# Strassen block products for the up and gate chunks of five feed-forward stages

## Chip, cores and metric

The kernel runs on one core of a Trainium2 chip. The metric is the device time of one execution in microseconds (us). Five compute engines take part: TensorE (PE, with its weight loads shown as PEld), VectorE (DVE), ScalarE (ACT), GpSimd (POOL) and SyncE (SP), which here issues the weight transfers.

## The reference

Four layers of width 1024 on 512 tokens in float32. Two of them end in a squared-relu feed-forward part, the other two have a SwiGLU feed-forward part ahead of the mixer and one behind it. What the change touches is the first matrix product of each:

```python
def _sq_relu_mlp(h, w_up, w_down):            # 1024 -> 4096 -> 1024
    u = jax.nn.relu(h @ w_up)
    return (u * u) @ w_down

def swiglu(x, w_gu, w_d):                     # 1024 -> 2 x 2816 -> 1024
    ...
    return (jax.nn.silu(gate) * up) @ w_d

def second_block(...):
    for i in range(DEPTH):                    # 2
        x = x + 0.5 * rms_norm(swiglu(rms_norm(x, g[0]), ffn_wgu[i, 0], ffn_wd[i, 0]), g[1])
        ...
        x = x + 0.5 * rms_norm(swiglu(rms_norm(x, g[4]), ffn_wgu[i, 1], ffn_wd[i, 1]), g[5])
```

## The kernel before

Every product is made of three: each operand is split into a rounded part (`hi`) and a rest (`lo`), and `three` issues hi·hi, hi·lo and lo·hi as three matmuls into one PSUM bank. The weights come from memory in chunks of 1 MB: 1024 rows by 256 columns for an up or gate chunk, 256 rows by 1024 columns for a down chunk. A chunk passes four engines. SP issues its load into one of two slots of `raw` (L291). ACT copies it to `whi` (L299), DVE subtracts to get `wlo` (L305), and PE multiplies it (`pe_chunk`, L309 to L311). `whi` and `wlo` have two slots too. The load of chunk n+2 waits until DVE has made `wlo` of chunk n, and ACT's copy of chunk n+2 waits until PE has finished chunk n.

The stages run in the order of PLAN: rg, f0, nsa, f1, s00, even, s01, s10, odd, s11, with a norm ahead of each, and post and store at the end. f0 and f1 are the squared-relu parts (16 groups of 256 columns, each one up chunk and one down chunk). The four s stages are the SwiGLU parts (11 groups of a gate chunk, an up chunk and a down chunk). `ffn_walk` fixes the order for every engine: gate and up of groups 0 and 1, down of 0, gate and up of 2, down of 1, and so on. Each engine runs its own program in that order and meets the others at semaphores.

In a gate or up chunk, PE makes two tiles of 128x512 (48 matmuls). DVE evicts a gate tile with a multiplication by `rstd` (L476), ACT takes silu (L426), POOL multiplies by `rstd` again (L458), DVE multiplies the up tile by that (L491), ACT rounds the product to `u_hi` (L434) and DVE makes `u_lo` (L496). In f1 the eviction is a relu (L480), and ACT squares. A down chunk is eight tiles of six matmuls. Tile m goes to bank m mod 4 of the half of PSUM that its group owns, DVE adds each to `fsum` or `x` (L517), and tile m=4 to 7 may start only when the add of tile m−4 is done, since it takes the same bank. The norms between the stages (L585 to L820) have PE, ACT, DVE and POOL work tile by tile; `pool_owed` (L687) is POOL's part there. `pool_even_early` and `pool_odd_early` prepare constants in `arena` for the mixers even and odd. POOL runs them ahead of its part of s00 and s10.

Of the kernel before, what the change touches and what calls it, by code (L numbers as in the profile page):

```python
# [20 lines left out]
P = 128  # L21
# [20 lines left out]
def build(nc, a, out):  # L42
    ctx = ExitStack()
    with ctx:
# [68 lines left out]
        LEFT, RIGHT = slice(0, S // 2), slice(S // 2, S)  # L113
        s_pe = sem("s_pe")
# [59 lines left out]
        def swi(l, i):  # L174
# [4 lines left out]
            return dict(gu=2, groups=NG2, w=[g, u], down=down, swiglu=True, dst=fsum)  # L179

# [87 lines left out]
        owed_no = {i: sum(s_[0] in ("norm", "post") and s_[1] is not None for s_ in PLAN[:i]) for i in range(len(PLAN))}  # L268
        swi_base = {n_: b_ - sum(FFN[m_]["groups"] for m_ in FFN if not FFN[m_]["swiglu"]) for n_, b_ in ffn_base.items()}
# [76 lines left out]
        def ffn_walk(e, name, gu, dn):  # L346
            f = FFN[name]
            G, per = f["groups"], f["gu"] + 1
            n0 = where[name]

            def n_gu(g):
                return n0 if g == 0 else n0 + f["gu"] + (g - 1) * per

            def n_dn(g):
                return n0 + f["gu"] + g * per + f["gu"] if g < G - 1 else n0 + G * per - 1
# [3 lines left out]
            dt = 2 * (2 * f["gu"] + 8)  # L359
            gu(0, n_gu(0), None, 0, 0)  # L360
            for g in (1, 2):
                gu(g, n_gu(g), None, 0, 0)
# [54 lines left out]
        def act_ffn(e, name):  # L417
            f, b, bs = FFN[name], ffn_base[name], swi_base[name]

            def gu(g, n, i, dn, dt):  # L420
                if f["swiglu"]:
# [28 lines left out]
            ffn_walk(e, name, gu, down)  # L450

        def pool_ffn(e, name):
            b = swi_base[name]

            def gu(g, n, i, dn, dt):
                for j in range(2):
                    e.wait_ge(silu_done, at(2 * (b + g) + j + 1, i, 4))
                    e.tensor_tensor(tmp[:, j, :], tmp[:, j, :], rstd[:, :], ALU.mult).then_inc(scaled, 1)  # L458
# [3 lines left out]
            ffn_walk(e, name, gu, down)  # L462

        def dve_ffn(e, name, stage):
# [3 lines left out]

            def gu(g, n, i, dn, dt):
                half = 4 * (g % 2)  # L470
# [22 lines left out]
                for j in range(2):  # L493
                    e.wait_ge(uhi_done, at(2 * (b + g) + j + 1, i, 4))
                    u = 2 * (g % 2) + j
                    e.tensor_tensor(u_lo[:, u, :], tmp[:, 2 + j, :], u_hi[:, u, :].bitcast(F32),  # L496
                                    ALU.subtract).then_inc(ulo_done, 1)
# [3 lines left out]
            def down(g, n, i, dn, dt):  # L501
                final = i is None and g == f["groups"] - 1
                half = 4 * (g % 2)
                for m in range(8):
                    if m == 4 and not final:
                        dve_lo(e, n + 1, i, dn, dt)
                    e.wait_ge(tiles_out, at(before[n] + m + 1, i, dt))
# [2831 lines left out]
```

## Time and profile before

| what | value |
|---|---|
| median of 3 runs | 3573.53 us (3571.29 to 3574.26) |
| span of the profiled execution | 3570.0 us |
| PE busy | 3490.7 us, 98% of the span |
| PEld busy | 2787.9 us, 78% |
| DVE busy | 1950.1 us, 55% |
| ACT busy | 1247.5 us, 35% |
| POOL busy | 439.1 us, 12% |

The span is one profiled execution, and the times of the runs contain some 3.5 us around it. A matmul's row shows the time from its start to its modelled end, and matmuls overlap, so PE's pace is read from the distance between starts.

### The profile page before, as it was taken

How to read it: one execution, taken by the hardware profiler on the slowest of the kernel's cores; microseconds unless marked ns; L12 is line 12 of the kernel's file. 1: busy time of each engine (PE TensorE's matmuls, PEld its weight loads, DVE VectorE, ACT ScalarE, POOL GpSimd, SP SyncE). 2: the span in 40 equal slices, each digit the busy share in tenths (PEclk: the TensorE clock that was granted, in tenths of full speed). 3: DMA queues.
4: the chain of work that ended last, by engine and by line, in shares of the span. 5: the costliest groups of instructions: out<-in, count | busy, mean ns of one | idle time of the engine just before them, and what ended most of it. 6: DMA issues, size and time to landing. Idle time of an engine off the chain costs nothing.

```text
span 3570.0 us, 47147 instructions
## 1 busy us (share of the span) xinstructions
PE 3490.7 (98%) x18751; PEld 2787.9 (78%) x18751; DVE 1950.1 (55%) x2686; ACT 1247.5 (35%) x1776; POOL 439.1 (12%) x351
## 2 busy tenths in 40 slices
PE   8999999999999999999999999999999999999998
PEld 6888888645888878887777788878888777778887
DVE  5655563465555565446577555555545534465545
ACT  5632232465422242223644422233223422243222
POOL 1220002010100021112023011111111000011101
PEclk9999999899999999999999999999999999999999
DMA  3332334100222222233100132323222222223231
GB/s 119 106 111 94 94 94 95 36 1 24 95 94 94 94 96 95 94 98 97 59 26 24 52 106 94 100 77 106 94 94 95 83 83 87 79 66 100 96 104 60
DMA packets 232554, 295.92 MB, mean 83 GB/s; under 512 B 21893, under 2 KB 201464, under 8 KB 232392
## 3 DMA queue, kind: packets, MB, share of 16 engines
q1 hardware_dynamic: 230864, 290.48, 25.6%
q0 software_dynamic: 1152, 3.05, 0.4%
q8 instruction: 115, 1.88, 0.2%
q14 instruction: 47, 0.39, 0.0%
q10 hardware_dynamic: 376, 0.12, 0.0%
HBM read 291.53 MB, written 2.10 MB: 82 GB/s over the span
## 4 chain that ended last, share of the span: by engine, by line
PE 90%; DVE 5%; ACT 3%; issue 1%; DMA 0%; SPq 0%; DVEq 0%; ACTq 0%
PE bank L309 26%; PE bank L311 26%; PE bank L310 26%; PE bank L338 1%; PE bank L340 1%; PE bank L339 1%; PE bank L3057 1%; DVE wlo L305 1%; PE bank L2458 1%; PE bank L1585 1%; PE bank L1500 1%; PE bank L1569 1%; ACT whi L299 1%; ACT fsum L1666 1%; PE bank L1599 0%
## 5 line engine op out<-in xcount | busy, mean ns | idle before, releaser
L309 PE MATMUL bank<-h_hi,whi 128*128 128x512 f32 x2748 | 1083.1, 394 | 22.2 <-DVE h_lo L789 9.9
L311 PE MATMUL bank<-h_hi,wlo 128*128 128x512 f32 x2748 | 1069.5, 389 | 0.0
L310 PE MATMUL bank<-h_lo,whi 128*128 128x512 f32 x2748 | 1069.3, 389 | 0.0
L299 ACT ACTIVATE whi<-raw 128x2048 fp32r<-128x2048 f32 x266 | 508.6, 1912 | 1245.1 <-PE bank L311 1192.7
L305 DVE TENSOR_TENSOR wlo<-raw,whi 128x2048 fp32r<-128x2048 f32 x266 | 612.9, 2304 | 323.5 <-ACT whi L299 323.4
L309 PEld LDWEIGHTS bank<-h_hi,whi 128*128 128x128 f32 x2748 | 517.0, 188 | 147.2 <-issue 31.4
L310 PEld LDWEIGHTS bank<-h_lo,whi 128*128 128x128 f32 x2748 | 517.1, 188 | 107.1 <-issue 3.6
L311 PEld LDWEIGHTS bank<-h_hi,wlo 128*128 128x128 f32 x2748 | 516.9, 188 | 107.4
L309 PE MATMUL bank<-u_hi,whi 128*128 128x512 f32 x1440 | 562.0, 390 | 4.6 <-DVE arena L3133 2.4
L310 PE MATMUL bank<-u_lo,whi 128*128 128x512 f32 x1440 | 560.8, 389 | 0.0
L311 PE MATMUL bank<-u_hi,wlo 128*128 128x512 f32 x1440 | 560.7, 389 | 0.0
L309 PEld LDWEIGHTS bank<-u_hi,whi 128*128 128x128 f32 x1440 | 270.4, 188 | 63.7 <-issue 4.3
L311 PEld LDWEIGHTS bank<-u_hi,wlo 128*128 128x128 f32 x1440 | 270.4, 188 | 56.2
L310 PEld LDWEIGHTS bank<-u_lo,whi 128*128 128x128 f32 x1440 | 270.4, 188 | 56.0 <-issue 0.2
L458 POOL TENSOR_TENSOR tmp<-tmp,rstd 128x512 f32<-128x512 f32 x88 | 175.4, 2014 | 1118.1 <-ACT tmp L426 1117.8
L517 DVE TENSOR_TENSOR fsum<-fsum,bank 128x512 f32<-128x512 f32 x316 | 212.1, 685 | 85.9 <-PE bank L311 84.8
L517 DVE TENSOR_TENSOR x<-x,bank 128x512 f32<-128x512 f32 x255 | 169.0, 683 | 51.7 <-PE bank L311 51.7
L491 DVE TENSOR_TENSOR tmp<-bank,tmp 128x512 f32<-128x512 f32 x88 | 60.8, 691 | 246.3 <-PE bank L311 210.8
L476 DVE TENSOR_TENSOR tmp<-bank,rstd 128x512 f32<-128x512 f32 x88 | 60.1, 690 | 229.2 <-PE bank L311 214.5
L434 ACT ACTIVATE u_hi<-tmp 128x512 fp32r<-128x512 f32 x88 | 55.7, 632 | 327.3 <-DVE tmp L491 327.3
L480 DVE SCALAR_TENSOR_TENSOR tmp<-bank,rstd 128x512 f32<-128x512 f32 x64 | 44.1, 691 | 181.3 <-PE bank L311 181.3
L438 ACT ACTIVATE tmp<-tmp 128x512 f32<-128x512 f32 x64 | 40.4, 632 | 256.6 <-DVE tmp L480 256.6
(441 smaller groups left out, 3095.6 us busy)
## 6 DMA issues: line engine op xcount, KB each, us to landing
raw<-in_ffn_wgu SPq DMA_DIRECT2D x88, 1024.0 KB, 5.0
raw<-in_ffn_wd SPq DMA_DIRECT2D x44, 1024.0 KB, 4.9
raw<-in_mlp_w_up SPq DMA_DIRECT2D x32, 1024.0 KB, 5.7
raw<-in_mlp_w_down SPq DMA_DIRECT2D x32, 1024.0 KB, 4.8
raw<-in_odd_w_in SPq DMA_DIRECT2D x24, 1024.0 KB, 5.1
raw<-in_even_w_in SPq DMA_DIRECT2D x13, 1024.0 KB, 5.3
raw<-in_rg_w_in SPq DMA_DIRECT2D x8, 1024.0 KB, 5.6
raw<-in_odd_w_out SPq DMA_DIRECT2D x8, 1024.0 KB, 5.0
```

The costliest lines, as they stand in the source:

```text
L299: e.activation(whi[:, n % 2, :], raw[:, n % 2, :], ACT.Copy).then_inc(hi_ready, 1)
L305: e.tensor_tensor(wlo[:, n % 2, :], raw[:, n % 2, :], whi[:, n % 2, :].bitcast(F32), ALU.subtract).then_inc(lo_ready, 1)
L309: pe.matmul(o, w_hi, r_hi, start=first, stop=False)
L310: pe.matmul(o, w_hi, r_lo, start=False, stop=False)
L311: return pe.matmul(o, w_lo, r_hi, start=False, stop=last)
L434: e.activation(u_hi[:, u, :], tmp[:, 2 + j, :], ACT.Copy).then_inc(uhi_done, 1)
L438: e.activation(tmp[:, 2 + j, :], tmp[:, j, :], ACT.Square)
L458: e.tensor_tensor(tmp[:, j, :], tmp[:, j, :], rstd[:, :], ALU.mult).then_inc(scaled, 1)
L476: ins = e.tensor_tensor(tmp[:, j, :], pbank[half + j][:, :], rstd[:, :], ALU.mult)
L480: ins = e.scalar_tensor_tensor(tmp[:, j, :], pbank[half + j][:, :], 0.0, rstd[:, :], ALU.max, ALU.mult)
L491: e.tensor_tensor(tmp[:, 2 + j, :], pbank[half + 2 + j][:, :], tmp[:, j, :], ALU.mult)\
L517: e.tensor_tensor(dst[:, m, :], dst[:, m, :], src[:, :], ALU.add).then_inc(added, 1)
```

## The change

In f1, s00, s01, s10 and s11 the up and gate chunks from group 3 on (13 chunks in f1, 16 in each s stage, 77 in all) are computed as a 2x2 block product by Strassen's scheme in Winograd's form: seven products of half the size in each dimension instead of eight. A chunk (1024 rows, 256 columns) is cut in four quarters of 512 rows and 128 columns, and the tokens in two halves of 256. One such product is 4 blocks of rows by 3 matmuls of 128x256, so a chunk is 84 matmuls of 128x256 (`pe_seven`) in place of 48 of 128x512.

The sums that the scheme needs are spread over the engines. POOL makes four sums of weights per chunk, each waiting for the one before (`pool_weights`, L444 to L450 of the new program, one of them written into `raw`); ACT then copies 2048 elements to `whi` and 1536 to `x_hi`, and DVE makes `wlo` and `x_lo` (L466). The token sums are made once per stage, from 8 DVE products, 8 POOL sums, 4 ACT copies and 4 DVE subtractions of 1792 elements, and stand in `th`, which lies in `arena`. `rstd` is already in the tokens, so POOL's scaling (L458) goes in these groups. The seven products are joined on the way out of PSUM: ACT copies the first to `snap`, and DVE adds tiles of 256 columns.

In the down chunks DVE makes `wlo` of the next chunk ahead of add m=1 instead of m=4, `x_lo` of the next gate chunk and both `u_lo` ahead of add m=3. Since `th` needs `arena`, `pool_even_early` and `pool_odd_early` move into the norm ahead of even and odd, behind `pool_owed`.

```diff
+        SEVEN = {"f1": 3, "s00": 3, "s01": 3, "s10": 3, "s11": 3}
+        def seven(name, g):
+            return name in SEVEN and SEVEN[name] <= g < FFN[name]["groups"]
...
+        PRODUCTS = (("m", 0, 0, TB11, 0), ("x", XS2, 0, T2, 1), ("x", XS3, 0, T3, 2), ("m", 0, 1, T1, 3),
+                    ("m", 4, 0, TB21, 0), ("m", 4, 1, T4, 2), ("x", XS4, 0, TB22, 3))
+        P_A, P_B, P_E, P_C, P_A2, P_E2, P_C2 = range(7)
...
+        def pool_weights(e, name, g, c, n, i, dn):
+            k = 2 * FFN[name]["gu"]
+            y = seven_no(name, g, c)
+            d = wsum[(y - seven_base[name]) % 2]
+            e.wait_ge(loaded[n % 2], at(landed[n], i, dn * 8))
+            if (y - seven_base[name]) % 2:
+                e.wait_ge(tiles_out, before[chunk_gu(name, SEVEN[name]) - 1])
+            if y > 1:
+                e.wait_ge(xlo_ready, at(y - 1, i, k))
+            e.tensor_tensor(d[:, XS3], quarter(n, 0, 0), quarter(n, 0, 1), ALU.subtract).then_inc(w_sum, 1)
+            e.wait_ge(w_sum, at(4 * y + 1, i, 4 * k))
+            e.tensor_tensor(quarter(n, 0, 1), quarter(n, 0, 1), quarter(n, 1, 1), ALU.add).then_inc(w_sum, 1)
+            e.wait_ge(w_sum, at(4 * y + 2, i, 4 * k))
+            e.tensor_tensor(d[:, XS2], quarter(n, 0, 1), quarter(n, 0, 0), ALU.subtract).then_inc(w_sum, 1)
+            e.wait_ge(w_sum, at(4 * y + 3, i, 4 * k))
+            e.tensor_tensor(d[:, XS4], quarter(n, 1, 0), d[:, XS2], ALU.subtract).then_inc(w_sum, 1)
...
+        def act_weights(e, name, g, c, n, i, dn, dt, middle=None):
+            k = 2 * FFN[name]["gu"]
+            y = seven_no(name, g, c)
+            e.wait_ge(tiles_out, at(before[n - 1], i, dt))
+            e.wait_ge(w_sum, at(4 * y + 4, i, 4 * k))
+            e.activation(whi[:, n % 2, :], raw[:, n % 2, :], ACT.Copy).then_inc(hi_ready, 1)
+            if middle:
+                middle()
+            e.activation(x_hi[:, n % 2, :, :, :], wsum[(y - seven_base[name]) % 2], ACT.Copy).then_inc(xhi_ready, 1)
...
+        def dve_weights_rest(e, name, g, c, n, i):
+            k = 2 * FFN[name]["gu"]
+            y = seven_no(name, g, c)
+            e.wait_ge(xhi_ready, at(y + 1, i, k))
+            e.tensor_tensor(x_lo[:, n % 2, :, :, :], wsum[(y - seven_base[name]) % 2], x_hi[:, n % 2, :, :, :].bitcast(F32), ALU.subtract)\
+                .then_inc(xlo_ready, 1)
...
+            pe.wait_ge(lo_ready, at(n + 1, i, dn))
+            for p, (src, q, m, t, r) in enumerate(PRODUCTS):
+                if p == P_B:
...
+                for j in range(4):
+                    if src == "m":
+                        w = (q + j) * 256 + m * P
+                        hi, lo = whi[:, s, w:w + P], wlo[:, s, w:w + P]
+                    else:
+                        hi, lo = x_hi[:, s, q, j, :], x_lo[:, s, q, j, :]
+                    first = j == 0 and p <= P_C
+                    last = j == 3
+                    pe.matmul(pbank[half + r][:, LEFT], hi, th[:, j, t, 1, :], start=first, stop=False, skip_group_check=True)
+                    pe.matmul(pbank[half + r][:, LEFT], hi, th[:, j, t, 0, :], start=False, stop=False, skip_group_check=True)
+                    ins = pe.matmul(pbank[half + r][:, LEFT], lo, th[:, j, t, 1, :], start=False, stop=last, skip_group_check=True)
+                ins.then_inc(tiles_out, 1)
...
+        def dve_tokens(e, name, stage):
+            sec, g0 = PLAN[stage - 1][2:4]
+            for k in range(4):
+                e.scalar_tensor_tensor(th_raw[:, k, TB11].rearrange("p j n -> p (j n)"), x[:, k, :], gain(sec, g0 + k),
+                                       rstd[:, :], ALU.mult, ALU.mult)
+                ins = e.scalar_tensor_tensor(th_raw[:, k, TB21:TB22 + 1, 0, :], halves(x[:, 4 + k, :]),
+                                             gain(sec, g0 + 4 + k), halves(rstd[:, :]), ALU.mult, ALU.mult)
+                if k % 2:
+                    ins.then_inc(t_scaled, 1)
...
+                e.tensor_tensor(v[T1], b12, v[TB11], ALU.subtract).then_inc(t_sum, 1)
+                e.tensor_tensor(v[T3], v[TB22], b12, ALU.subtract).then_inc(t_sum, 1)
...
+                e.activation(th[:, k, :, 1, :], th_raw[:, k, :, 0, :], ACT.Copy).then_inc(t_hi, 1)
...
+                e.tensor_tensor(th[:, k, :, 0, :], th_raw[:, k, :, 0, :], th[:, k, :, 1, :].bitcast(F32), ALU.subtract)\
+                    .then_inc(t_lo, 1)
...
+                def joined(c):
+                    e.wait_ge(seven_act, at(a0 + 2 * c + 1, i, 2 * acts))
+                    e.tensor_tensor(snap[:, c, :], part(c, P_B), snap[:, c, :], ALU.add).then_inc(seven_dve, 1)
+                def last_quarter(c):
+                    d = tmp[:, 2 * c + 1, RIGHT]
+                    if c == 0 and not f["swiglu"]:
+                        e.wait_ge(uhi_done, at(2 * (b + g - 1) + 2, i, 4))
+                    src = part(c, P_E)
+                    step(3 * c + 1)
+                    e.tensor_tensor(d, src, snap[:, c, :], ALU.add).then_inc(seven_dve, 1)
+                    src = part(c, P_C)
+                    step(3 * c + 2)
+                    e.tensor_tensor(d, src, d, ALU.add).then_inc(seven_dve, 1)
+                def outer(c, p, d, signal):
+                    e.tensor_tensor(d, part(c, p), snap[:, c, :], ALU.add).then_inc(signal, 1)
+                if f["swiglu"]:
+                    dve_lo(e, n + 1, i, dn, dt)
+                joined(0)
+                last_quarter(0)
+                if f["swiglu"]:
+                    dve_weights_rest(e, name, g, 1, n + 1, i)
+                outer(0, P_E2, tmp[:, 1, LEFT], gate_done)
+                outer(0, P_C2, tmp[:, 0, RIGHT], gate_done)
+                if not f["swiglu"]:
+                    return
+                dve_lo(e, n + 2, i, dn, dt)
+                joined(1)
+                last_quarter(1)
+                src = part(1, P_A2)
+                e.wait_ge(seven_act, at(a0 + 2, i, 2 * acts))
+                e.tensor_tensor(tmp[:, 2, LEFT], src, tmp[:, 0, LEFT], ALU.mult)
+                outer(1, P_E2, tmp[:, 3, LEFT], seven_dve)
+                outer(1, P_C2, tmp[:, 2, RIGHT], seven_dve)
+                e.wait_ge(silu_done, at(2 * (bs + g) + 1, i, 4))
+                step(7)
+                e.tensor_tensor(tmp[:, 3, :], tmp[:, 3, :], tmp[:, 1, :], ALU.mult).then_inc(prod_done, 1)
+                e.wait_ge(silu_done, at(2 * (bs + g) + 2, i, 4))
+                step(8)
+                e.tensor_tensor(tmp[:, 2, RIGHT], tmp[:, 2, RIGHT], tmp[:, 0, RIGHT], ALU.mult).then_inc(prod_done, 1)
...
+                early = seven(name, g + 1)
+                first = 1 if early else 4
                 for m in range(8):
-                    if m == 4 and not final:
+                    if m == first and not final:
                         dve_lo(e, n + 1, i, dn, dt)
+                    if m == first + 2 and seven(name, g + 2):
+                        dve_weights_rest(e, name, g + 2, 0, n + 1, i)
+                    if m == 3 and early:
+                        u_low(g + 1, i)
...
                 pool_owed(e, stage)
+                if PLAN[stage + 1] == ("even",):
+                    pool_even_early(e, chain)
+                elif PLAN[stage + 1] == ("odd",):
+                    pool_odd_early(e, chain)
```

DVE in s00, the unrolled groups behind the loop, before. This is one group from the eviction of the gate tiles on: the up tiles, `u_lo`, then the eight adds of a down chunk.

```order
L476 TENSOR_TENSOR tmp<-bank,rstd 128x512 x2
L305 TENSOR_TENSOR wlo<-raw,whi 128x2048
L491 TENSOR_TENSOR tmp<-bank,tmp 128x512 x2
L496 TENSOR_TENSOR u_lo<-tmp,u_hi 128x512 x2
L517 TENSOR_TENSOR fsum<-fsum,bank 128x512 x4
L305 TENSOR_TENSOR wlo<-raw,whi 128x2048
L517 TENSOR_TENSOR fsum<-fsum,bank 128x512 x4
L305 TENSOR_TENSOR wlo<-raw,whi 128x2048
```

In this row the `u_lo` pair stands ahead of all adds and a `wlo` in the middle and at the end. Behind the change the same place, from the last evictions of an up chunk on, reads:

```order
L730 TENSOR_TENSOR tmp<-bank,arena 128x256 x2
L751 TENSOR_TENSOR tmp<-tmp 128x512
L754 TENSOR_TENSOR tmp<-tmp 128x256
L819 TENSOR_TENSOR fsum<-fsum,bank 128x512
L336 TENSOR_TENSOR wlo<-raw,whi 128x2048
L819 TENSOR_TENSOR fsum<-fsum,bank 128x512 x2
L466 TENSOR_TENSOR x_lo<-tmp,x_hi 128x1536
L760 TENSOR_TENSOR u_lo<-tmp,u_hi 128x512 x2
L819 TENSOR_TENSOR fsum<-fsum,bank 128x512 x5
```

Ahead of the fourth add there now stand `wlo`, `x_lo` and both `u_lo`, and the `wlo` in the row's last place before now stands in the next chunk.

POOL from the last groups of s00 into the norm ahead of even, before: the scalings of the last two groups, `pool_owed`, and the first steps of even.

```order
L458 TENSOR_TENSOR tmp<-tmp,rstd 128x512 x4
L687 TENSOR_TENSOR tmp<-tmp 128x512 x4
L1955 MEMSET rz 128x1 x2
L1957 DMA arena<-in_rwkv_w_up 64x512
L1958 DMA arena<-in_rwkv_a_up 64x512
L1959 DMA arena<-in_rwkv_g_up 128x512
```

POOL at that place behind the change, from the four sums of the last up chunk on:

```order
L444 TENSOR_TENSOR sums_b<-raw 128x512
L446 TENSOR_TENSOR raw<-raw 128x4x128
L448 TENSOR_TENSOR sums_b<-raw 128x512
L450 TENSOR_TENSOR sums_b<-raw,sums_b 128x512
L991 TENSOR_TENSOR tmp<-tmp 128x512 x4
L2250 DMA arena<-in_diff_lam 128x256
L2252 IOTA arena 128x512
L2254 TENSOR_SCALAR arena<-arena 128x512
L2255 TENSOR_TENSOR arena<-arena 128x512
L2256 MEMSET arena 64x64
L2258 TENSOR_SCALAR arena<-arena 128x512 x4
L2263 MEMSET rz 128x1 x2
```

Where a group's two scalings stood, two chunks' eight sums now stand, each with operands in SBUF alone, and between `pool_owed` (L687 before, L991 now) and even's first steps come the load, the iota and the six sums of `pool_even_early` that stood ahead of s00.

## Rows read from the trace of the kernel before

**Rows 1.** Page, busy time and chain that ended last: by engine, then by line.

```profile
PE 3490.7 (98%) x18751; PEld 2787.9 (78%) x18751; DVE 1950.1 (55%) x2686; ACT 1247.5 (35%) x1776; POOL 439.1 (12%) x351
PE 90%; DVE 5%; ACT 3%; issue 1%; DMA 0%; SPq 0%; DVEq 0%; ACTq 0%
```

**Rows 2.** Busy time by stretch (PE, PEld, DVE, ACT, POOL, PEclk, DMA, GB/s): f1; s00.

```profile
940.00:1290.00 350.00, 348.42 (x1542) 288.32 (x1541) 203.94 (x242) 108.58 (x122) 6.49 (x4) 1.00 0.29 93
1330.00:1630.00 300.00, 300.00 (x1325) 248.49 (x1324) 149.93 (x160) 75.94 (x69) 41.48 (x21) 1.00 0.30 96
```

**Rows 3.** Timeline of PE (start, us): 512 columns in s00, 256 in a norm.

```profile
1330.20 0.39 PE L310 MATMUL bank<-h_lo,whi 128*128 128x512 f32 x1
...
1339.72 0.39 PE L310 MATMUL bank<-h_lo,whi 128*128 128x512 f32 x1
...
1638.10 0.28 PE L310 MATMUL bank<-h_lo,whi 128*128 128x256 f32 x1
...
1638.58 0.28 PE L311 MATMUL bank<-h_hi,wlo 128*128 128x256 f32 x1
```

**Rows 4.** Groups by line and shape: busy us, mean ns of one, idle before.

```profile
L305 DVE TENSOR_TENSOR wlo<-raw,whi 128x2048 fp32r<-128x2048 f32 x266 | 612.9, 2304 | 323.5 <-ACT whi L299 323.4
L517 DVE TENSOR_TENSOR fsum<-fsum,bank 128x512 f32<-128x512 f32 x316 | 212.1, 685 | 85.9 <-PE bank L311 84.8 <-DVE fsum L517 0.3
L496 DVE TENSOR_TENSOR u_lo<-tmp,u_hi 128x512 fp32r<-128x512 f32 x152 | 104.5, 687 | 25.9 <-ACT u_hi L439 21.5
L759 DVE SCALAR_TENSOR_TENSOR tmp<-fsum,par,rstd 128x512 f32<-128x512 f32 x43 | 32.0, 744 | 4.0 <-ACT rstd L606 4.0
L2858 DVE TENSOR_TENSOR rz<-bank,arena 128x256 f32<-128x256 f32 x8 | 3.3, 414 | 0.0
L299 ACT ACTIVATE whi<-raw 128x2048 fp32r<-128x2048 f32 x266 | 508.6, 1912 | 1245.1 <-PE bank L311 1192.7 <-PE bank L340 48.1 <-DMA raw<-in_rg_w_in 4.4
```

**Rows 5.** Timeline of DVE in s00: start, duration, idle before.

```profile
1405.57 2.29 DVE L305 TENSOR_TENSOR wlo<-raw,whi 128x2048 fp32r<-128x2048 f32 x1 [1.26 <-ACT whi L299]
1409.21 0.69 DVE L491 TENSOR_TENSOR tmp<-bank,tmp 128x512 f32<-128x512 f32 x1 [1.35 <-PE bank L311]
...
1438.20 2.29 DVE L305 TENSOR_TENSOR wlo<-raw,whi 128x2048 fp32r<-128x2048 f32 x1 [1.17 <-ACT whi L299]
```

**Rows 6.** POOL beside them, and one line's durations (ns min/median/max).

```profile
1406.13 4.12 POOL L458 TENSOR_TENSOR tmp<-tmp,rstd 128x512 f32<-128x512 f32 x2 [28.52 <-ACT tmp L426]
L458 POOL TENSOR_TENSOR tmp<-tmp,rstd x88: 1284/1298/2885, 1307.8 to 3521.1; 128x512 f32<-128x512 f32 x88
```

**Rows 7.** Timeline of POOL, then DVE, at the end of odd.

```profile
3168.65 8.45 POOL L687 TENSOR_TENSOR tmp<-tmp 128x512 f32<-128x512 f32 x4 [11.82 <-ACT tmp L585]
...
3169.18 3.38 DVE L305 TENSOR_TENSOR wlo<-raw,whi 128x2048 fp32r<-128x2048 f32 x1
3172.48 0.68 DVE L3190 TENSOR_TENSOR arena<-bank,arena 128x512 f32<-128x512 f32 x1
3173.20 1.07 DVE L3191 TENSOR_TENSOR fsum<-fsum,arena 128x512 f32<-128x512 f32 x1
```

**Rows 8.** SP's issue of a load behind that `wlo`, and loads (us to landing).

```profile
1440.67 0.37 SPq L291 DMA_DIRECT2D raw<-in_ffn_wgu  x1
raw<-in_ffn_wgu SPq DMA_DIRECT2D x88, 1024.0 KB, 5.0
```

**Rows 9.** Timeline of POOL: constants for even and for odd.

```profile
1297.32 2.35 POOL L1946 TENSOR_SCALAR arena<-arena 128x512 f32<-128x512 f32 x1
1299.75 1.29 POOL L1947 TENSOR_TENSOR arena<-arena 128x512 f32<-128x512 f32 x1
...
1301.34 6.21 POOL L1950 TENSOR_SCALAR arena<-arena 128x512 f32<-128x512 f32 x4
...
2422.59 3.27 POOL L2994 TENSOR_SCALAR arena<-arena 128x512 f32<-128x512 f32 x1
```

**Rows 10.** Waits of PE on DVE in the norms: total us, times, longest.

```profile
PE bank L309 <- DVE h_lo L789: 9.9, 12, 1.1
```

More of the change, by code:

```diff
@@ L358, in ffn_walk @@
                 turns -= 1
-            dt = 2 * (2 * f["gu"] + 8)
+            dt = before[n_gu(5)] - before[n_gu(3)]
             gu(0, n_gu(0), None, 0, 0)
             for g in (1, 2):
+                if g == 2 and name in SEVEN:
+                    between()
                 gu(g, n_gu(g), None, 0, 0)
@@ L404, in gu @@
                         continue
+                    if seven(name, g):
+                        if c == 0 and g == SEVEN[name]:
+                            pe.wait_ge(t_lo, 4 * t_no[name] + 4)
+                        pe_seven(pe, name, g, c, n + c, half, free, i, dn)
+                        continue
                     pe_chunk(pe, n + c, KT, 2, h_hi, h_lo, lambda m: pbank[half + 2 * c + m][:, :], free, i, dn)
@@ L445, in down @@
                     e.preload_act_table_set(LOGEXP)
+                if f["swiglu"] and seven(name, g + 2):
+                    return
                 if i is not None or g < f["groups"] - 1:
@@ L469, in gu, with u_low @@
+            def u_low(g, i):
+                for j in range(2):
+                    e.wait_ge(uhi_done, at(2 * (b + g) + j + 1, i, 4))
+                    u = 2 * (g % 2) + j
+                    e.tensor_tensor(u_lo[:, u, :], tmp[:, 2 + j, :], u_hi[:, u, :].bitcast(F32),
+                                    ALU.subtract).then_inc(ulo_done, 1)
             def gu(g, n, i, dn, dt):
+                if seven(name, g):
+                    gu_seven(g, n, i, dn, dt)
+                    return
                 half = 4 * (g % 2)
@@ L492, in gu @@
                             .then_inc(prod_done, 1)
[L493 to L497, printed above, removed]
+                u_low(g, i)
+                if g == 0:
+                    if name in SEVEN:
+                        dve_tokens(e, name, stage)
                 if g == 0 and not f["swiglu"]:
@@ L3229, in _ @@
                     pool_owed(pool, stage)
[L3230 removed]
+                elif step[0] == "ffn" and (FFN[step[1]]["swiglu"] or step[1] in SEVEN):
                     pool_ffn(pool, step[1])
                 elif step[0] == "norm":
[L3233 removed]
+                    pool_norm(pool, stage, chain)
                     nxt = PLAN[stage + 1]
```

187 lines of the change are left out of this document (164 added, 23 removed).

## The prediction

> **What bounds the kernel now.** I read the page's busy times and its chain of waits first. PE is busy 98% of the span, and the chain that ended last runs through PE for 90% of it, with DVE at 5% and ACT at 3% [rows 1]. Next comes the busy time by stretch: in s00 PE has no gap at all in 300 us, DVE works half of them and POOL 41 us; in f1 PE is busy 348.4 of 350 us, DVE 203.9 and POOL 6.5, and the granted clock is 1.00 in both [rows 2]. So time is won in these stages only by giving PE less to do, and lost as soon as DVE, ACT or POOL can't follow. Then I read PE's pace from the timeline, the cost of each form of instruction from the groups, and one stretch of DVE and POOL side by side.
>
> **What PE saves.** In s00 42 matmuls of 512 columns lie between 1330.20 and 1339.72, which is 226.7 ns each; four steps of 256 columns lie between 1638.10 and 1638.58, 119 to 120 ns each, and I take 119 [rows 3]. Before, a chunk is 48 x 226.7 = 10.88 us, now 84 x 119 = 10.00 us: 0.886 us less. With 16 chunks in each s stage and 13 in f1 that is 77 x 0.886 = **−68 us**. The narrow pace is seen in bursts of six only; at 129.5 ns (10.88 / 84) the saving is gone.
>
> **Costs of the new instructions.** Of DVE's forms with two operands in SBUF, 2048 elements take 2.29 us and 512 take 0.69 [rows 4, 5]; along the line between them 1536 (`x_lo`) are 1.76 and 1792 (a quarter of `th`'s rest) 2.03. A 256-wide read of PSUM is 0.41 to 0.42, an add of 512 is 0.69, the product with a gain 0.74 [rows 4]. A POOL sum of 512 in SBUF is 1.29 when alone and up to 2.89 beside DVE [rows 6].
>
> **What happens when POOL and DVE meet.** POOL's pair of scalings from 1406.13 on took 4.12 us instead of about 2.7, and began inside DVE's `wlo` of 1405.57 to 1407.86; the next DVE instruction, which reads PSUM, ran its 0.69 us at 1409.21 while POOL was at work [rows 5, 6]. At the end of odd it is the other way: `wlo` at 3169.18 took 3.38 instead of 2.29 and an SBUF add 1.07 instead of 0.69 beside four POOL sums, which took 8.45 [rows 7]. So an instruction of DVE with two SBUF operands and one of POOL wait for each other. A meeting that POOL wins costs DVE between nothing and a whole POOL sum less the joint, 1.15; `wlo` lost 1.09 and the add 0.38 [rows 7]. I take the middle, 0.57.
>
> **The down chunk of an s stage** is where this matters. Tile m=7 of a down chunk needs the bank of tile m=3, so the add of m=3 must be done when PE has made seven tiles: 7 x 6 x 0.2267 = 9.52 us after it finished the up chunk. Before, `u_lo`, three adds and the add of m=3 stand there; now DVE's row from that moment is: last up tile 0.42, the two products 0.69 and 0.42, add m=0 0.69, `wlo` 2.29, adds m=1 and 2 1.37, `x_lo` 1.76, both `u_lo` 1.37, add m=3 0.69, in sum 9.70. Instructions that follow each other overlap by some 0.08 (3.38 from 3169.18 on ends at 3172.56, and the next starts at 3172.48 [rows 7]); eight joints, some of them with a wait instead, leave about 9.3. The spare is 0.2 us. In the same window POOL makes sums: `wlo` early in the up chunk releases the load of the next up chunk (as `wlo` ending at 1440.49 released the issue at 1440.67 [rows 5, 8]), the load lands 5.0 us later [rows 8], ACT can't copy before the sums are made, and the four sums in a chain take at least 4 x 1.29 plus joints, 5.6 us. They begin some 8 us into the up chunk and so reach 4 us or more into the down chunk, beside the products, `wlo` and, when POOL was held up itself, `x_lo`. Four meetings at 0.57 are 2.3 us, less the 0.2 spare is a stall of 2.1 us. The range of that is 0 (all meetings fall beside instructions that read PSUM) to 4 x 1.15 − 0.2 = 4.4. Seven downs of a stage have the whole row (those ahead of a group whose gate chunk is split in this way, from group 3 to the last but one), and the one after the last such costs half a microsecond at most: 7 x 2.1 + 0.4 = 15.1 a stage, **+60 us** in four (0 to +124). Two chunks of saving, 1.77 us, are the point at which a group comes out even.
>
> **f1** has one chunk of the kind per group, without the two products (1.11 us), so its row has a spare near 1.3 us. With one chunk's sums instead of two POOL is idle half of the time. Meetings of 0 to 2.3 us less that spare leave 0 to 1.0 us, and I take 0.6: 12 downs, **+7 us** (0 to +12).
>
> **The token sums, once a stage.** DVE has 8 x 0.74 and 4 x 2.03 = 14 us more, and POOL's eight sums of 512 in between meet them (8 x 0.57 = 4.6). An s stage hides that: its group repeats after 32.63 us (`wlo` at 1405.57 and 1438.20 [rows 5]) and DVE has half of it free [rows 2]. I put 1 us there for each (0 to 5). In f1 DVE is busy 203.9 of 350 us [rows 2], which over 16 groups of 21.8 us is 9.1 us free in each; 18.6 us in about one group leave **+9 us** (0 to 14). Together +13.
>
> **The constants of even and odd** move into norms. Those norms are where DVE, not PE, sets the time: PE waited 12 times, 9.9 us in all, for `h_lo` [rows 10]. Even's constants are 2.35 + 1.29 + 6.21 = 9.85 us of POOL, odd's longest step is 3.27 [rows 9], and they now stand between `pool_owed` and the rest of the norm, beside DVE's `h_lo` chain of instructions with two SBUF operands. What each lost to the other would be 0 to 9.85 and 0 to some 4; I take about half, 5 + 2 = **+7 us**. What they leave in s00 and s10 is no gain, as POOL is far from the bound there [rows 2].
>
> POOL's scalings that go (two per group) and the shorter ACT path are nothing on PE's path: PE had no gap in s00 [rows 2]. ACT's additional 1536 elements per chunk, by 1.91 us for 2048 [rows 4], are below 1.9 us, and ACT is busy a quarter of that stretch [rows 2].
>
> **Sum.** −68 + 60 + 7 + 13 + 7 = **+19 us**. The profiled span is 3570.0 us, and the runs' median lies 3.5 us above it, so I expect a span near 3589 and a median of **3593 us**.
>
> **Rivals.**
> - *The meetings fall into gaps* (faster). POOL's sums end before DVE's row begins, or wait themselves instead of being waited for, so that a down stalls 0.3 us: 4 x 7 x 0.3 = 8 in place of 60, f1 0, token sums 8, constants 4: −68 + 20 = −48, 3525; with half of the middle stall it is about 3550. I write it as 3545. For it: in the stretch shown DVE ran undelayed and POOL bore the loss [rows 5, 6]. Against it: the row has no slack of its own, and a late POOL makes the next `whi` late. It decides below 2.0 us of meetings a group.
> - *POOL becomes the pace* (much slower). Eight sums a group at 2.4 us, half way between 1.29 and the largest row with its joint, are 19 us beside loads that wait for each other; if each down stalls 4.4 us, that is +124 in place of +60: 3657.
> - *The narrow matmuls don't keep 119 ns in long runs.* At 129.5 ns nothing is saved and 3661 is the result. For it: PEld is busy 78% of the span already [rows 1], and there are 84 weight loads instead of 48. Against it: nothing in the six-bursts shows a growing step [rows 3].
> The Trainium skill, "TensorE: Matmul & The Clock Gate", section "Back-to-back issue gap", speaks against the change: it gives some 81 ns for 128 columns and 131 ns for 512 in a stream of loads and matmuls, so 256 columns would by an estimate on a line between them be 98 ns, and a chunk 84 x 98 = 8.2 us against 48 x 131 = 6.3, a loss of 1.9 us each. The trace has 227 ns at 512 columns [rows 3], so here the page's figures don't hold and the rows decide.
> - *Nothing to measure:* stalls near 1.4 us a group and small starts, within 7 us of 3573.5.
>
> **How the numbers follow.** 0.2% is 7 us, about what a measurement of this kernel can tell from no change. My forecast (slower, 3581 to 3625) has 0.40, the gaps rival 0.32, POOL as the pace 0.12, the wide pace 0.04, nothing to measure 0.12. So faster 0.32, same 0.12, slower 0.56. The range leaves out the far ends of the first and last cases, 0.1 each: 3538 to 3645. The forecast's own range is 3581 to 3625.
>
> **What would show it.** In the profile behind: starts of 128x256 matmuls about 119 ns apart in the s stages (the narrow-pace step); PE waiting at tile m=7 of downs for the add of m=3, some 2 us each, in the waits of PE on `fsum` (the stall step), with DVE's `wlo`, `x_lo` or `u_lo` longer than 2.29, 1.76 and 0.69 there; POOL's sums at more than 1.29 us; PE gaps in the first three groups of f1; and the norm ahead of even longer by some 5 us. PE with no gap in the downs would make the forecast wrong on the fast side; PE waiting for `wlo` at the start of gate or up chunks would make it wrong on the slow side.

## The result

The changed kernel takes 3589.45 us, median of 4 runs (3586.43 to 3594.08), and the kernel before, beside it, 3572.41 us (3570.41 to 3574.26). The ratio is 1.0049, with a 95% interval of 1.0035 to 1.0063: 17 us slower. The forecast was 3593 us and slower. The profiled spans are 3589.8 and 3570.0 us, 19.8 us apart.

Page of the changed kernel, busy time of each engine; it answers to [rows 1].

```profile
PE 3452.3 (96%) x21523; PEld 2859.4 (80%) x21523; DVE 2330.7 (65%) x3150; ACT 1431.2 (40%) x2021; POOL 950.5 (26%) x635
```

PE has 38 us less to do than in [rows 1] and is busy for 96% of a longer span, so 58 us more have become idle time. Two views say where it went. First the waits of PE in the changed kernel: who was waited for, us in all, times, the longest. The waits for `h_lo`, in the norms, are about as in [rows 10]; new are those for `fsum` and `x`, which are adds in down chunks, and one for `wlo`.

```profile
PE bank L340 <- DVE fsum L819: 42.6, 42, 2.2
PE bank L340 <- DVE h_lo L1097: 11.1, 12, 1.4
PE bank L340 <- DVE wlo L336: 9.2, 11, 4.0
PE bank L340 <- DVE x L819: 6.8, 13, 4.4
```

Then the timeline of PE in s01: start, duration, and idle time before. From 2232.75 to 2242.29 there are 81 steps from one 256-column matmul to the next, 117.8 ns each, so the narrow pace holds in long runs. In the down chunk ahead of them PE stops twice, at the first matmuls of its tiles m=5 and m=7.

```profile
2226.02 0.50 PE L340 MATMUL bank<-u_hi,whi 128*128 128x512 f32 x1 [0.66 <-DVE fsum L819]
...
2230.08 0.50 PE L340 MATMUL bank<-u_hi,whi 128*128 128x512 f32 x1 [1.03 <-DVE fsum L819]
...
2232.75 0.28 PE L502 MATMUL bank<-th,whi 128*128 128x256 f32 x1
...
2242.29 0.28 PE L502 MATMUL bank<-th,whi 128*128 128x256 f32 x1
```

The idle time is counted from the modelled end of the matmul before. From start to start the two steps are 0.82 and 1.19 us longer than 227 ns, and that is what is lost; below, "stall" means this. The timelines of DVE and POOL at the same place show why:

```profile
2218.89 1.74 DVE L751 TENSOR_TENSOR tmp<-tmp 128x512 f32<-128x512 f32 x1
2220.55 1.51 DVE L754 TENSOR_TENSOR tmp<-tmp 128x256 f32<-128x256 f32 x1
2221.99 0.68 DVE L819 TENSOR_TENSOR fsum<-fsum,bank 128x512 f32<-128x512 f32 x1
2222.59 2.78 DVE L336 TENSOR_TENSOR wlo<-raw,whi 128x2048 fp32r<-128x2048 f32 x1
2225.29 1.27 DVE L819 TENSOR_TENSOR fsum<-fsum,bank 128x512 f32<-128x512 f32 x2
2226.48 1.75 DVE L466 TENSOR_TENSOR x_lo<-tmp,x_hi 128x1536 fp32r<-128x1536 f32 x1
2228.15 1.28 DVE L760 TENSOR_TENSOR u_lo<-tmp,u_hi 128x512 fp32r<-128x512 f32 x2
2229.36 3.20 DVE L819 TENSOR_TENSOR fsum<-fsum,bank 128x512 f32<-128x512 f32 x5
...
2218.78 1.30 POOL L444 TENSOR_TENSOR sums_b<-raw 128x512 f32<-128x512 f32 x1 [2.87 <-DMA raw<-in_ffn_wgu]
2220.16 1.63 POOL L446 TENSOR_TENSOR raw<-raw 128x512 f32<-128x512 f32 x1
2221.86 1.35 POOL L448 TENSOR_TENSOR sums_b<-raw 128x512 f32<-128x512 f32 x1
2223.29 3.20 POOL L450 TENSOR_TENSOR sums_b<-raw,sums_b 128x512 f32<-128x512 f32 x1
```

The two products take 1.74 and 1.51 where 0.69 and 0.42 were put down, `wlo` 2.78 instead of 2.29: beside POOL's sums DVE loses 2.6 us ahead of add m=1. Tile m=5 waits for that add; tile m=7 waits for add m=3, behind `x_lo` and `u_lo`. The adds, which read PSUM, are at 0.68 to 0.69 beside the same sums.

Each stage can be measured from the end of its first down chunk's last add to that of its last down chunk. A group of an s stage was 32.64 us, and without any stall it is 30.71 (e1_late, below): the saving is 1.93 us a group, 0.965 a chunk.

| stretch (us) | before | after | e1_late | e2_small_sums |
|---|---|---|---|---|
| f1, first to last down | 315.58 | 315.57 | 310.76 | 309.82 |
| s00 | 304.70 | 305.93 | 289.59 | 289.23 |
| s01 | 304.70 | 304.96 | 289.55 | 289.23 |
| s10 | 304.70 | 304.93 | 289.20 | 289.23 |
| s11 | 304.70 | 304.04 | 289.51 | 289.23 |
| f1's end to first down of s00 | 63.12 | 65.10 | 65.07 | 65.07 |

In the s stages the whole saving is taken back by stalls and slow steps behind them (last section).

### The profile page after: what moved, and what is told of

Its sections match the earlier page's. It is cut to its first block and busy times, and to the rows that moved or that the text cites. A ratio compares the mean times of both kernels' runs of the same rounds, so it can differ in the third digit from the quotient of the medians.

```text
span 3589.8 us, 54969 instructions
## 1 busy us (share of the span) xinstructions
PE 3452.3 (96%) x21523; PEld 2859.4 (80%) x21523; DVE 2330.7 (65%) x3150; ACT 1431.2 (40%) x2021; POOL 950.5 (26%) x635
## 5 line engine op out<-in xcount | busy, mean ns | idle before, releaser
L340 PE MATMUL bank<-h_hi,whi 128*128 128x512 f32 (+1 forms) x1516 | 604.6, 399 | 22.9 <-DVE h_lo L1097 11.1
L342 PE MATMUL bank<-h_hi,wlo 128*128 128x512 f32 (+1 forms) x1516 | 590.8, 390 | 0.0
L341 PE MATMUL bank<-h_lo,whi 128*128 128x512 f32 (+1 forms) x1516 | 590.6, 390 | 0.0
L340 PEld LDWEIGHTS bank<-h_hi,whi 128*128 128x128 f32 x1516 | 286.4, 189 | 100.0 <-issue 32.1
L501 PE MATMUL bank<-th,whi 128*128 128x256 f32 x1232 | 345.9, 281 | 0.0
L502 PE MATMUL bank<-th,whi 128*128 128x256 f32 x1232 | 345.4, 280 | 0.0
L503 PE MATMUL bank<-th,wlo 128*128 128x256 f32 x1232 | 345.0, 280 | 0.0
L342 PEld LDWEIGHTS bank<-h_hi,wlo 128*128 128x128 f32 x1516 | 286.3, 189 | 59.9
L501 PE MATMUL bank<-th,x_hi 128*128 128x256 f32 x924 | 258.5, 280 | 0.2 <-DVE x_lo L466 0.2
L502 PE MATMUL bank<-th,x_hi 128*128 128x256 f32 x924 | 258.0, 279 | 0.0
L503 PE MATMUL bank<-th,x_lo 128*128 128x256 f32 x924 | 257.7, 279 | 0.0
L501 PEld LDWEIGHTS bank<-th,whi 128*128 128x128 f32 x1232 | 233.2, 189 | 2.1
```

What stands on the lines that cost most here:

```text
L340: pe.matmul(o, w_hi, r_hi, start=first, stop=False)
L341: pe.matmul(o, w_hi, r_lo, start=False, stop=False)
L342: return pe.matmul(o, w_lo, r_hi, start=False, stop=last)
L501: pe.matmul(pbank[half + r][:, LEFT], hi, th[:, j, t, 1, :], start=first, stop=False, skip_group_check=True)
L502: pe.matmul(pbank[half + r][:, LEFT], hi, th[:, j, t, 0, :], start=False, stop=False, skip_group_check=True)
L503: ins = pe.matmul(pbank[half + r][:, LEFT], lo, th[:, j, t, 1, :], start=False, stop=last, skip_group_check=True)
```

## The experiments

**1. The row ahead of the adds.** The theory says that what stands between the last products and add m=3 is the price; the rival, that the weights, made later, hold up the next gate chunk. e1_late:

```diff
-                first = 1 if early else 4
+                first = 4
+                rest = 5 if early else 6
...
-                    if m == first + 2 and seven(name, g + 2):
+                    if m == rest and seven(name, g + 2):
...
-                    if m == 3 and early:
+                    if m == 6 and early:
                         u_low(g + 1, i)
```

> The changed kernel with one thing moved: in the down chunks DVE makes wlo of the next chunk ahead of add m=4 (as in the kernel before), x_lo ahead of add m=5 and both u_lo ahead of add m=6, so nothing but the adds stands between the last products and the add of m=3. Theory (DVE's row ahead of the adds stalls PE at tiles m=5 and m=7): PE's waits for fsum in the s stages, some 51 us and some 16 us of narrow and wide matmuls at half pace behind the longer of them, go nearly wholly, as do f1's 0.5 us a group: about 3525 us, 3515 to 3540. Rival (the weights come too late for the next gate chunk, since wlo and x_lo stand later): PE then waits for wlo or x_lo at the start of gate chunks instead, and the time stays within 3565 to 3600.

Measured: 3520.21 us (3518.67 to 3522.53), ratio to before 0.9858 [0.9841, 0.9874]. No wait for `fsum` is left among the larger ones, and none at a gate chunk took its place. Waits of PE in this kernel, the first two:

```profile
PE bank L340 <- DVE h_lo L1098: 11.2, 12, 1.4
PE bank L340 <- DVE wlo L336: 9.2, 11, 4.0
```

Its timeline of DVE in one down chunk of s01. Successive groups' products start 30.70 us apart (2191.14, 2221.84). The small product still takes 1.52 instead of 0.42, but the four adds come ahead of `wlo` and PE does not wait.

```profile
2191.14 0.68 DVE L751 TENSOR_TENSOR tmp<-tmp 128x512 f32<-128x512 f32 x1
...
2221.84 0.68 DVE L751 TENSOR_TENSOR tmp<-tmp 128x512 f32<-128x512 f32 x1
2222.44 1.52 DVE L754 TENSOR_TENSOR tmp<-tmp 128x256 f32<-128x256 f32 x1
2223.89 1.27 DVE L820 TENSOR_TENSOR fsum<-fsum,bank 128x512 f32<-128x512 f32 x2
2225.71 0.69 DVE L820 TENSOR_TENSOR fsum<-fsum,bank 128x512 f32<-128x512 f32 x1 [0.55 <-PE bank L342]
2227.07 0.69 DVE L820 TENSOR_TENSOR fsum<-fsum,bank 128x512 f32<-128x512 f32 x1 [0.67 <-PE bank L342]
2227.67 2.35 DVE L336 TENSOR_TENSOR wlo<-raw,whi 128x2048 fp32r<-128x2048 f32 x1
```

So the change is worth 51 us, against the kernel before that ran beside it, once three steps of DVE stand elsewhere.

**2. POOL's part in it.** e2_small_sums keeps the changed kernel's order and cuts POOL's sums to 8 of 128 columns, so it leaves out most of their work. One of the four cuts is shown, and the zeros for the rest:

```diff
-            e.tensor_tensor(d[:, XS3], quarter(n, 0, 0), quarter(n, 0, 1), ALU.subtract).then_inc(w_sum, 1)
+            e.tensor_tensor(d[:, XS3, :, 0:8], quarter(n, 0, 0)[:, :, 0:8], quarter(n, 0, 1)[:, :, 0:8], ALU.subtract).then_inc(w_sum, 1)
...
+                    chain(e.memset(sums_b[:, :, :, :], 0.0))
+                    chain(e.memset(tmp[:, 4:7, :], 0.0))
```

> The changed kernel with POOL's four sums per chunk cut to 8 of 128 columns each (their chain, signals and everything downstream stay; the rest of the sums is zero, so this kernel leaves out most of the sums' work). Theory (meetings of POOL and DVE lengthen DVE's row by some 2 us per down chunk): DVE's products run 0.69 and 0.42, wlo 2.29, and the waits of PE for fsum fall from 51 us to below 12 us: about 3535 us, 3525 to 3550. Rival (the row is too long by itself, whatever POOL does): waits of more than 1 us per down chunk stay, and the time is 3565 to 3590.

Measured: 3517.23 us (3513.25 to 3519.18), ratio 0.9847 [0.9831, 0.9864], a larger gain than expected. With the order unchanged, the s stages run as in e1_late (table above). The groups of DVE by line (busy us, mean ns of one) show the products, first in the changed kernel, then in e2_small_sums, where the same two lines are L754 and L757:

```profile
L751 DVE TENSOR_TENSOR tmp<-tmp 128x512 f32<-128x512 f32 x32 | 37.6, 1175 | 0.0
L754 DVE TENSOR_TENSOR tmp<-tmp 128x256 f32<-128x256 f32 x32 | 40.9, 1277 | 0.0
L730 DVE TENSOR_TENSOR tmp<-bank,arena 128x256 f32<-128x256 f32 x154 | 65.3, 424 | 152.8 <-PE bank L503 152.8
```

```profile
L754 DVE TENSOR_TENSOR tmp<-tmp 128x512 f32<-128x512 f32 x32 | 22.2, 693 | 0.0
L757 DVE TENSOR_TENSOR tmp<-tmp 128x256 f32<-128x256 f32 x32 | 14.9, 467 | 0.0
```

The products fall from 1175 and 1277 ns to 693 and 467. The eviction at L730, with one operand in PSUM, has 424 ns with or without POOL's sums (425 at L733 of e2_small_sums). So the row just fits by itself, as worked out, and the meetings push it over; in the s stages either cure is enough. The Trainium skill, "SBUF — State Buffer", section "Who interferes with whom", calls the port pair that VectorE and GpSimd share an exclusive lock; these rows agree: the products with two operands in SBUF grow beside POOL's sums, and the eviction with one does not.

In f1 nothing changed: a group is 21.32 us in both kernels, against 20.82 in e1_late. There POOL is not the cause (see f1 in the next section).

**3. The scheme without f1.** e3_no_f1:

```diff
-        SEVEN = {"f1": 3, "s00": 3, "s01": 3, "s10": 3, "s11": 3}
+        SEVEN = {"s00": 3, "s01": 3, "s10": 3, "s11": 3}
```

> The changed kernel with f1 left as it was before, the scheme in the four s stages alone. From the trace f1's token sums cost 8.2 us up to its first down chunk and 6.4 us in the second group, and its 13 groups give back 6.4 us: the theory expects 8 us less than the changed kernel, about 3581 us (3577 to 3585). Rival (part of the 8.2 us ahead of f1 comes from elsewhere, such as the stages ahead of it): 3585 to 3590.

Measured: 3580.3 us (10 runs, 3570.28 to 3586.51), ratio 1.0019 [1.0008, 1.0031]. It is 9 us below the changed kernel, as expected, but not all of the 9 is f1. Between the two profiled executions f1 with its start differs by 5.8 us, and another 5.0 lie in the s stages (1219.9 against 1214.9 us in sum), where the programs are the same. So f1 is a loss of about 6 us, since its start costs 12.2 (below) and its 13 groups bring 6.4, and the rest is scatter.

**4. Which step makes which stall.** e5_wlo_early is e1_late with `wlo` back ahead of add m=1:

```diff
-                first = 4
+                first = 1 if early else 4
                 rest = 5 if early else 6
```

> The kernel of the late weights (e1_late) with wlo back ahead of add m=1, as in the changed kernel; x_lo and both u_lo stay behind add m=4 and m=5. Theory (the wait of PE at tile m=5 comes of the products and wlo, lengthened by POOL, ahead of add m=1, and the one at m=7 of x_lo and u_lo): waits of about 0.8 us at tile m=5 come back in some 7 down chunks of each s stage, none over 1.5 us, and no 256-column matmul behind them runs at half pace: 3520 plus 4 x 5 is about 3540 us, 3528 to 3546. Rival (all of the loss hangs on wlo alone): 3570 or more. Rival (x_lo and u_lo alone): within 3 us of 3520.

Measured: 3538.74 us (3532.43 to 3542.03), ratio 0.9898 [0.9881, 0.9914]. The waits for `fsum` are back in part, and only the short ones, at tile m=5:

```profile
PE bank L340 <- DVE fsum L820: 10.0, 18, 0.8
```

So of some 69 us between the changed kernel and e1_late, `wlo`'s place is 19, and that of `x_lo` and `u_lo`, with `wlo` early, 51. The fourth order (`wlo` late, the other two early) was not run, so the shares hold for this order of steps alone.

**5. The starts.** In e1_late f1 and the s stages still wait at their starts. e4_starts spreads the token work:

```diff
+                if g == 0 and not f["swiglu"]:
+                    dve_lo(e, n + f["gu"] + 1, i, dn, dt)
+                if name in SEVEN and (g == 0 or g == 1 and not f["swiglu"]):
+                    dve_tokens(e, name, stage, (2 * g, 2 * g + 1))
...
+                    if g == 1 and name in SEVEN:
+                        dve_tokens(e, name, stage, (2, 3))
                     for j in range(2):
                         e.wait_ge(tiles_out, at(before[n + 1] + j + 1, i, dt))
...
+                    if m == 4 and g == 1 and name in SEVEN and not f["swiglu"]:
+                        dve_tokens_rest(e, name, (2, 3))
```

> The kernel of the late weights (e1_late) with the start of each stage spread: f1 makes wlo of its next chunk ahead of the token products, the eight token products stand half behind group 0 and half in group 1, and in f1 two of the four subtractions for the tokens' rest stand in the down chunk of group 1 ahead of wlo. Theory (what is left at the starts is DVE's token work standing ahead of wlo and of adds): f1's wait of 4.2 us for wlo with 2 to 3 us of half pace behind it goes, most of its wait of 4.5 us for an add with 2.7 us at half pace goes, and about 1 us goes in each s stage: 3520 less 6, 6 and 4 is about 3504 us, 3498 to 3512. Rival (POOL's token sums, now later, hold up ScalarE's copies and so the first split chunk): 3513 to 3525, with new waits of PE at the first 256-column matmul of a stage.

Measured: 3537.97 us (3535.93 to 3540.72), ratio 0.9899 [0.9882, 0.9915]: 18 us slower than e1_late, a miss. f1 became 3.4 us shorter, but each s stage waits at its first down chunk:

```profile
PE bank L340 <- DVE fsum L818: 18.6, 4, 4.7
```

Half of the token products stood ahead of the up tiles' products, and so ahead of `u_lo` and the first adds. It is the same mistake as in the change itself. e6_starts_down puts them behind add m=3 in the s stages:

```diff
-                    if g == 1 and name in SEVEN:
-                        dve_tokens(e, name, stage, (2, 3))
                     for j in range(2):
...
+                    if m == 4 and g == 0 and name in SEVEN and f["swiglu"]:
+                        dve_tokens(e, name, stage, (2, 3))
```

> The kernel of the late weights (e1_late) with f1's start as in e4_starts (wlo ahead of the token products, two of the four subtractions later), and in the s stages the second half of the token products not ahead of the up tiles' products of group 1, as in e4_starts, but in the first down chunk behind add m=3. Theory (in e4_starts PE waited 4.7 us in each first down chunk because the token products stood ahead of u_lo; behind the add of m=3 nothing on PE's path waits for them): f1 gives back about 6 us, each s stage about 1 us: 3510 us, 3504 to 3516. Rival (POOL's later token sums hold up ScalarE's copies of the tokens, and with them the wlo of the next chunk): 3516 to 3530.

Measured: 3520.9 us (3514.49 to 3521.96), ratio 0.9853 [0.9837, 0.9869], no better than e1_late. The 4.7-us waits are gone, but an s stage is 290.8 us instead of 289.5: what f1 won, the s stages lost. The expected gain of 1 us there did not come. e8_f1_start takes f1's part alone:

```diff
+                if name in SEVEN and f["swiglu"] and g == 0:
+                    dve_tokens(e, name, stage, range(4))
+                if name in SEVEN and not f["swiglu"] and g < 2:
+                    dve_tokens(e, name, stage, (2 * g, 2 * g + 1))
...
-                    if m == 4 and g == 0 and name in SEVEN and f["swiglu"]:
-                        dve_tokens(e, name, stage, (2, 3))
```

> The kernel of the late weights (e1_late) with only f1's start as in e4_starts and e6_starts_down; the s stages start as in e1_late. In e6_starts_down f1 became 4.0 us shorter and each s stage 1.3 us longer than in e1_late. Theory (the two add up, being in separate stages): 3520 less 4 is 3516 us, 3513 to 3519. Rival (f1's gain is taken back ahead of its first down chunk): 3519 to 3523.

Measured: 3516.71 us (3512.51 to 3519.14), ratio 0.9844 [0.9831, 0.9858]. It is the fastest of the kernels that compute everything, 54 us below the kernel before. The 3.5 us to e1_late are as expected, but no more than the scatter of stretches that are the same in all kernels (next section).

**6. How much cover POOL has.** e7_sums_twice makes three of the four sums twice in e1_late:

```diff
+            for m in range(2):
+                sums(3 + m)
+                e.tensor_tensor(d[:, XS2], quarter(n, 0, 1), quarter(n, 0, 0), ALU.subtract).then_inc(w_sum, 1)
```

> The kernel of the late weights (e1_late) with three of POOL's four sums per chunk made twice (7 instead of 4 in the chain). Theory (with x_lo and u_lo behind the adds POOL has cover: eight sums are some 14 of the 30.7 us of a group, and what they cost DVE no longer stands ahead of an add): PE waits under 1 us a group more, 3520 to 3545 us. Rival (POOL's chain is close to being the pace): sums of 26 us a group and more waits of wlo for them, each group 2 us longer or more: above 3580 us.

Measured: 3680.34 us (3675.06 to 3684.24), ratio 1.0306 [1.0289, 1.0324]: 160 us more, far beyond the theory, and on the rival's side. Waits of PE in this kernel, the first three:

```profile
PE bank L508 <- DVE fsum L827: 59.8, 43, 1.9
PE bank L508 <- DVE tmp L731: 32.9, 28, 1.2
PE bank L508 <- ACT arena L617: 24.6, 18, 2.9
```

None is for `wlo`. ACT's timeline shows one way in which late sums reach PE:

```profile
1481.25 1.91 ACT L464 ACTIVATE whi<-raw 128x2048 fp32r<-128x2048 f32 x1 [9.18 <-POOL sums_b L457]
1483.07 0.36 ACT L617 ACTIVATE arena<-bank 128x256 f32<-128x256 f32 x1
```

ACT stands 9.18 us at `whi` for POOL's last sum, and the copy of the first product out of PSUM (L617), for which PE waits until 1483.49, is queued behind it. What sets the time is a circle through POOL. The rows show POOL, DVE and POOL again in this kernel; the last row is POOL in e1_late.

```profile
1455.63 4.60 POOL L449 TENSOR_TENSOR tmp<-raw 128x512 f32<-128x512 f32 x2 [9.67 <-DMA raw<-in_ffn_wgu]
1483.20 2.29 DVE L336 TENSOR_TENSOR wlo<-raw,whi 128x2048 fp32r<-128x2048 f32 x1 [3.28 <-ACT whi L464]
1490.84 4.59 POOL L449 TENSOR_TENSOR tmp<-raw 128x512 f32<-128x512 f32 x2 [9.62 <-DMA raw<-in_ffn_wgu]
...
2212.01 1.30 POOL L444 TENSOR_TENSOR tmp<-raw 128x512 f32<-128x512 f32 x1 [14.85 <-DMA raw<-in_ffn_wgu]
```

POOL makes both chunks' sums from 1455.63 to 1481.22, 25.6 us with no wait in between (the rival had 26). `whi` and `wlo` follow at once and end at 1485.49, SP issues the next gate chunk's load at 1485.69, and when it has landed POOL begins again at 1490.84, 9.62 us after its last sum. The two make 35.2 us, which is the distance to the next group's first sum, where an unstalled group of PE has 30.71. 4.5 us in some nine groups of four stages are the 160 us. In e1_late POOL waits 14.85 us for that load instead of 9.62, and another 2.7 for the up chunk's: that is its cover, under 8 us a group, while the second sums cost over 12. So its cover is smaller than its busy share says.

## Why the prediction held, point by point

| term | predicted | measured | how |
|---|---|---|---|
| PE's saving | −68 | −74 | 77 x 0.965 |
| down chunks of the s stages | +60 | +62 | the four stages' differences, +1.2, +0.3, +0.2 and −0.7, and 64 x 0.965 given back, less 0.3 a stage for starts |
| groups of f1 | +7 | +6 | 12 x (21.32 − 20.82) |
| starts | +13 | +21 | f1 5.8 + 6.4, s 4 x 2.3 |
| constants of even and odd | +7 | about +1 | PE's waits in the norm |
| sum | +19 | +16 | spans +19.8 |

Some 3 us more of the difference between the spans lie in stretches whose instructions did not change. The stretch up to f0's first down chunk, the same in all kernels, is 215.8 to 218.5 us long. The 3.5 us that the forecast put between span and median is no fixed price: an execution of the changed kernel takes 1.7 us more than its own span, and the profiled one, 3591.5 us, was among the longer, so the median lies 0.35 us below the span shown.

- **Narrow pace**: right, 117.8 ns against 119.
- **Down chunks of the s stages**: right in mechanism, and in size partly by luck. The 0.42-us product loses 0.86 us on average and the 0.69 one 0.49 (1277 and 1175 ns), `wlo` 0.5 in the stretch shown: about 2 us, where four meetings at the middle, 0.57, made 2.3. The middle had no ground but being the middle. The loss lies ahead of add m=1. That makes a stall at m=5, which the working had not seen, and the one at m=7 is smaller for it (0.82 and 1.19 where 2.1 was worked out for m=7). Counted from start to start, the stalls of the four stages are some 50 us, 10 below the +60; the other 12 are slow steps behind them, most of it half pace (last section), which was not in the sum. So the +62 is nearer to the +60 than the working deserves. In the second rival, 2.4 us is not half way between 1.29 and 2.89; that is 2.1, and eight sums are then 17 us instead of 19, which changes no price.
- **f1**: the size is right and the cause wrong. It was put down to meetings; e2_small_sums, which takes them away, leaves the 21.32 us. DVE and then ACT in f1 of the changed kernel:

```profile
1082.24 0.69 DVE L819 TENSOR_TENSOR x<-x,bank 128x512 f32<-128x512 f32 x1 [1.07 <-PE bank L342]
1083.46 2.29 DVE L336 TENSOR_TENSOR wlo<-raw,whi 128x2048 fp32r<-128x2048 f32 x1 [0.54 <-ACT whi L457]
...
1081.53 1.90 ACT L457 ACTIVATE whi<-raw 128x2048 fp32r<-128x2048 f32 x1
```

ACT begins `whi` only behind the relu of the up chunk, so `wlo`, at its full speed, ends at 1085.75, and PE starts tile m=7 of such a chunk 0.37 us late. e1_late, where `wlo` stands behind the adds, has a group of 20.82. A step that waits for another engine stood in DVE's row, and the working had only counted DVE's own time.

- **Starts**: the step that failed most. In the working the token work was measured against DVE's free time in a group. The trace shows that its place decides. PE waits 4.0 us for `wlo`, which stands behind eight token products, the last three of them beside POOL at 1.78 us; then 4.4 us for an add behind the four subtractions, which took 12.23 us instead of 8.1:

```profile
936.43 1.78 DVE L511 SCALAR_TENSOR_TENSOR th_raw<-x,par,rstd 128x512 f32<-128x512 f32 x1
...
939.84 1.77 DVE L511 SCALAR_TENSOR_TENSOR th_raw<-x,par,rstd 128x512 f32<-128x512 f32 x1
941.54 3.35 DVE L336 TENSOR_TENSOR wlo<-raw,whi 128x2048 fp32r<-128x2048 f32 x1
...
961.78 12.23 DVE L539 TENSOR_TENSOR th<-th_raw,th 128x1792 fp32r<-128x1792 f32 x4
```

f1 alone lost 12.2 us there, 5.8 up to its first down chunk and 6.4 in the group behind it (28.15 us instead of 21.76); some 3 of them are half pace behind the waits. The s stages lose 2.0 ahead of their first down chunk (table) and 0.3 behind it (e1_late's 289.5 against 289.2).
- **Constants**: mis-sized, at most 1.3 us in the norm ahead of even instead of 5. There PE waited 3.5 us for `h_lo` (before, 2.2). Both engines gave way a little: POOL's four steps took 7.11 us instead of 6.21 [rows 9], and DVE's product with a gain lost 0.35 (1.09 instead of 0.74 [rows 4]) where they met.

```profile
1649.24 7.11 POOL L2258 TENSOR_SCALAR arena<-arena 128x512 f32<-128x512 f32 x4
...
1651.22 1.09 DVE L1067 SCALAR_TENSOR_TENSOR tmp<-fsum,par,rstd 128x512 f32<-128x512 f32 x1
```

With odd, the runs' scatter is larger than the effect.
- **Rivals**: the gaps rival named the right condition; e1_late meets it by order instead of by luck and reaches the 3525 worked out there less 5. POOL as the pace did not decide here, but e7_sums_twice shows that it is not far off, and that the loads that wait for each other, which this rival named, are the way.

## What to carry to other kernels

Where an engine that isn't the bound empties the bound engine's buffers, write down its whole row ahead of each emptying step, and put everything that nobody waits for yet behind it: here three steps moved by a few places turn 17 us lost into 51 us won. An instruction's price alone is not its price beside another engine: here a product of 0.42 us lost 0.86 beside POOL's sums, and a `wlo` of 2.29 lost 0.5. An engine's share of busy time does not show whether a step's place hurts; the same token products cost an s stage a wait of 4.7 us in one place and some 2 us in another.

## What was not expected of the hardware

Behind some stalls PE runs at half pace for a while. Busy time by stretch of the changed kernel in s00 (PE, PEld, DVE, ACT, POOL, PEclk): the first stretch is behind a wait of 1.01 us, the second behind one of 2.04, the third a little later.

```profile
1402.60:1404.00 1.40, 1.40 (x9) 1.18 (x8) 1.36 (x4) 0.06 (x1) 0.00 (x0) 1.00 0.00 0
1436.20:1438.80 2.60, 2.60 (x12) 2.31 (x11) 1.46 (x3) 1.18 (x1) 0.00 (x0) 0.50 0.00 0
1440.00:1443.00 3.00, 3.00 (x28) 3.00 (x27) 2.39 (x3) 1.73 (x2) 0.00 (x0) 1.00 0.00 0
```

At a granted clock of 0.50, the lower of the two levels, 1.2 GHz, starts of 512 columns are 0.42 us apart and of 256 columns 0.21; at 1.00 they are 0.23 and 0.12. That makes a stall of 2.2 us cost up to 3.9 (2.21, at 1469.83 in s00, and 1.72 behind it), and is the larger part of why the groups of s00 differ, from 32.3 to 35.0 us. It does not follow the length of the wait alone: in s10 of the changed kernel a wait of 2.04 us before 2567.69 is followed by a granted clock of 1.00, and so is one of 2.05 us in e6_starts_down, shown here.

```profile
949.50:952.00 2.50, 2.50 (x12) 2.00 (x12) 2.50 (x4) 0.00 (x0) 2.50 (x3) 1.00 0.00 0
```

What decides between the two is left open.
